# ScalarE makes the copies of the transposed input, and its high and low parts read it in PSUM

## The reference, cut to what matters

```python
h = rmsnorm(x, g_mix_pre)        # x * rsqrt(mean(x*x) + eps) * gain
q_a, k_a, v_a, q_r, k_r, v_r, g_r, gate_a, gate_r = split_in(h @ w_in)
...
x = x + rmsnorm(merged @ w_out, g_mix_post)
```

## Time and profile before

| | |
|---|---|
| median of 3 runs | 982.86 us |
| lowest, highest | 982.62, 986.0 us |
| the profiled execution | 982.29 us |
| its span | 980.6 us |
| its mean granted clock of TensorE | 0.999 |

### The profile page before, as it was taken

How to read it: one execution, slowest core, us unless ns; L and a number is a source line. 1 busy time by engine, 2 the same in 40 slices (tenths; PEclk the granted TensorE clock), 3 DMA queues, 4 the chain that set the end, 5 groups by cost and what they waited for, 6 DMA issues and landing times.

```text
span 980.6 us, 18692 instructions
## 1 busy us (share of the span) xinstructions
PE 973.6 (99%) x7286; PEld 954.4 (97%) x7286; DVE 632.6 (65%) x1246; ACT 396.9 (40%) x695; POOL 85.7 (9%) x140
## 2 busy tenths in 40 slices
PE   9999999999999999999999999999999999999998
PEld 7999999999999999999999999999999999999997
DVE  6554676757665633435458899535996469976772
ACT  4334533434343522223455555424453234544352
POOL 2123212112100000010003000000000000030000
PEclk9999999999999999999999999999999999999999
DMA  8434221222222232246603533521334213366221
GB/s 215 135 114 130 81 68 55 66 76 68 59 68 66 76 92 81 76 127 186 182 3 118 204 86 87 151 66 47 109 99 128 72 48 109 98 202 192 87 55 44
DMA packets 166213, 98.68 MB, mean 101 GB/s; under 512 B 14656, under 2 KB 162528, under 8 KB 165872
## 3 DMA queue, kind: packets, MB, share of 16 engines
q1 hardware_dynamic: 159904, 79.19, 28.6%
q0 software_dynamic: 4336, 16.67, 4.8%
q10 hardware_dynamic: 1888, 1.64, 0.6%
HBM read 86.79 MB, written 10.75 MB: 99 GB/s over the span
## 4 chain that ended last, share of the span: by engine, by line
PE 97%; DVE 1%; DMA 1%; SPq 0%; issue 0%; ACT 0%; DVEq 0%
PE acc L683 37%; PE acc L960 11%; PE acc L961 11%; PE acc L962 11%; PE small L960 6%; PE small L961 6%; PE small L962 6%; PE small L829 1%; PE small L875 1%; PE small L846 1%; PE small L879 1%; PE small L838 1%; PE small L877 1%; PE acc L791 1%; DMA x_row<-in_x_sample 1%; PE small L1117 1%
## 5 line engine op out<-in xcount | busy, mean ns | idle before, releaser
L683 PE MATMUL acc<-xh,whi 128*128 128x288 f32 x720 | 158.9, 302 | 0.1
L683 PE MATMUL acc<-xh,wlo 128*128 128x288 f32 x720 | 153.4, 294 | 0.0
L683 PE MATMUL acc<-xl,whi 128*128 128x288 f32 x720 | 153.4, 294 | 0.0
L1143 ACT ACTIVATE whi<-raw 128x1024 fp32r<-128x1024 f32 (+1 forms) x61 | 61.1, 1002 | 197.7 <-PE acc L683 196.4
L683 PEld LDWEIGHTS acc<-xh,whi 128*128 128x128 f32 x720 | 113.9, 188 | 5.9 <-issue 4.7
L683 PEld LDWEIGHTS acc<-xh,wlo 128*128 128x128 f32 x720 | 115.0, 188 | 0.0
L683 PEld LDWEIGHTS acc<-xl,whi 128*128 128x128 f32 x720 | 115.0, 188 | 0.0
L1965 DVE TENSOR_TENSOR wlo<-raw,whi 128x512 fp32r<-128x512 f32 (+2 forms) x93 | 80.9, 871 | 50.0 <-ACT whi L1359 34.3
L960 PE MATMUL acc<-yh,whi 128*128 128x288 f32 x360 | 107.0, 297 | 0.0
L962 PE MATMUL acc<-yh,wlo 128*128 128x288 f32 x360 | 106.1, 295 | 0.0
L1636 DVE TENSOR_TENSOR wlo<-raw,whi 128x1024 fp32r<-128x1024 f32 (+1 forms) x63 | 73.0, 1158 | 44.4 <-ACT whi L1143 43.4
(11 more groups left out here) (326 smaller groups left out, 2396.1 us busy)
## 6 DMA issues: line engine op xcount, KB each, us to landing
raw<-in_w_in SPq DMA_DIRECT2D x92, 256.0 KB, 3.2
raw<-in_w_ffn_gate SPq DMA_DIRECT2D x44, 256.0 KB, 3.4
raw<-in_w_ffn_up SPq DMA_DIRECT2D x44, 256.0 KB, 4.2
raw<-in_w_ffn_down SPq DMA_DIRECT2D x32, 256.0 KB, 3.7
res<-x_scratch POOLq DMA_DIRECT2D x16, 288.0 KB, 4.2
raw<-in_w_branch_ret SPq DMA_DIRECT2D x16, 256.0 KB, 3.0
raw<-in_w_out SPq DMA_DIRECT2D x16, 256.0 KB, 4.4
raw<-in_w_ffn_down SPq DMA_DIRECT2D x16, 192.0 KB, 3.8
```

What stands on the lines that cost most here:

```text
L683: ins = nc.tensor.matmul(acc[:, a, hf, 0:HALF], w[:, s, at:at + P], x(k)[:, hf * HALF:(hf + 1) * HALF], start=first and n == 0 and m == 0, ...
L1143: nc.scalar.activation(whi[:, s, 0:n], raw[:, s, 0:n], ACT.Copy).then_inc(hi_ready, 1)
```

## The change

PSUM halves get a name, `xt_of(k)`. ScalarE's xh reads the block there instead of in `x_t`, and VectorE's xl too. The copy to `x_t` moves from VectorE to ScalarE: that of block k - 1 stands behind xh of block k and waits until xl of block k - 1 has been made. VectorE copies the gains first. TensorE's hook runs behind the matmuls of unit 0 in a step, not ahead of them.

```diff
+        def xt_of(k):
+            return small[:, 1024 * (k % 2):1024 * (k % 2) + ROWS]
...
                 for step in range(KD + lag):
-                    if before is not None:
-                        before(step)
...
                         if k == KD - 1:
                             ins.then_inc(unit_done, 1)
+                        if n == 0 and before is not None:
+                            before(k)
...
             for k in range(KD):
-                act.wait_ge(xt_copied, k + 1)
-                nc.scalar.activation(xh[:, k, :], x_t[:, k, :], ACT.Copy,
-                                     scale=gains[:, k:k + 1]).then_inc(xh_ready, 1)
+                act.wait_ge(xt_psum, k + 1)
+                nc.scalar.activation(xh[:, k, :], xt_of(k), ACT.Copy, scale=gains[:, k:k + 1]).then_inc(xh_ready, 1)
+                if k > 0:
+                    act.wait_ge(xl_ready, k)
+                    nc.scalar.activation(x_t[:, k - 1, :], xt_of(k - 1), ACT.Copy).then_inc(xt_copied, 1)
                 if k == 0:
                     split_hi(unit(U_KV))
                 elif k == 3:
                     split_hi(unit(U_KV + 1))
                 elif k == KD - 2:
                     row_squares(0)
+            act.wait_ge(xl_ready, KD)
+            nc.scalar.activation(x_t[:, KD - 1, :], xt_of(KD - 1), ACT.Copy).then_inc(xt_copied, 1)
...
-            for k in range(KD + 1):
-                if k < KD:
-                    dve.wait_ge(xt_psum, k + 1)
-                    nc.vector.tensor_copy(x_t[:, k, :], small[:, 1024 * (k % 2):1024 * (k % 2) + ROWS]).then_inc(xt_copied, 1)
+            dve.wait_ge(gain_t, 1)
+            nc.vector.tensor_copy(gains[:, 0:KD], acc[:, 0, 0, 0:KD]).then_inc(gain_ready, 1)
+            dve.wait_ge(gain_ready, 1)
+            for k in range(KD):
+                dve.wait_ge(xh_ready, k + 1)
+                nc.vector.scalar_tensor_tensor(xl[:, k, :], xt_of(k), gains[:, k:k + 1], xh[:, k, :].bitcast(F32),
+                                               ALU.mult, ALU.subtract).then_inc(xl_ready, 1)
                 if k == 0:
-                    dve.wait_ge(gain_t, 1)
-                    nc.vector.tensor_copy(gains[:, 0:KD], acc[:, 0, 0, 0:KD]).then_inc(gain_ready, 1)
-                    dve.wait_ge(gain_ready, 1)
-                if k > 0:
-                    dve.wait_ge(xt_copied, k)
-                    dve.wait_ge(xh_ready, k)
-                    nc.vector.scalar_tensor_tensor(xl[:, k - 1, :], x_t[:, k - 1, :], gains[:, k - 1:k],
-                                                   xh[:, k - 1, :].bitcast(F32), ALU.mult, ALU.subtract).then_inc(xl_ready, 1)
-                if k == 1:
                     split_lo(unit(U_KV))
-                elif k == 4:
+                elif k == 3:
                     split_lo(unit(U_KV + 1))
```

## The result

The changed kernel took 984.07 us in the median of 22 executions (983.35 to 986.56), beside 982.73 us for the kernel before; the ratio is 1.0016, 95% interval 1.001 to 1.0023. So it is slower by 1.3 us, about a fourth of the 0.5% that the prediction called telling. The forecast was 984.1 us. It is closer than its reasons are: the 22 executions are not spread around 984. In 12 of them the granted clock of TensorE was 0.999 or 1.00 and the time 983.35 to 984.2 us (median 983.5); in 10 it was 0.998 or less and the time 985.2 to 986.56 us (median 985.9). The median lies at the upper edge of the first group, because nearly half of the executions fell into the second. That it meets the forecast to 0.03 us is in part luck, and both groups have to be explained. The profiled execution, 985.44 us with a span of 983.8, is one of the second group.

The account below looks back on a forecast made before the run. The prediction took TensorE to bound the kernel. Waits of 0.16, 0.67 and 0.67 us less an old wait of 0.30 made +1.2 us, on the median of 982.86 a forecast of 984.1 us, range 982.0 to 986.5.

Parts of the forecast that it names:

- The bound, and a plain shift behind 32 us: Whole kernel: TensorE bounds, busy 973.6 of 980.6 us; early delay of 1.2 us then carries through as a plain shift.
- The power that I had watched near 36 us: GpSimd's power, ending some 0.4 us ahead of the matmuls reading it; a new wait there would show the forecast wrong.
- Prices of the instructions: Split of x: xh from PSUM 0.74 us, the copy on ScalarE 0.65 us, xl 811 ns.
- The ring: Transposes to the next transposes through ScalarE's xh and the earlier block's copy: 2.31 us a turn.
- T(4) and T(5): TensorE's five transposes each of blocks 4 and 5: forecast to wait 0.67 us each for ScalarE's copy.
- T(6) and T(7): TensorE's transposes of blocks 6 and 7, both units running: forecast no wait, 0.11 us to spare.
- T(2), forecast +0.16: TensorE's transposes of block 2: forecast to start at 10.31 instead of 10.15 us, waiting for block 0's copy.
- The step that the first weights land by 7.92 us: Ahead of the weights' high part on ScalarE: transfers there at 7.92 us at the latest, the high part following at 8.02.
- c(0): The copy of block 0 on ScalarE, behind xh of block 1: forecast to start at 9.62 and end at 10.27 us.
- The clock: Rival: waits around blocks 2 to 7 drop TensorE to 1.2 GHz, about 5 blocks for +4.9 us, 988 or more; chance 0.05.
- The first rival: ScalarE quicker than taken, transposes of blocks 4 and 5 hardly waiting: -0.3 to +0.5 us; chance 0.13.
- the second: ScalarE slower, its PSUM reads taking 1.0 us beside VectorE and TensorE: +3.9 to +4.6 us; chance 0.19.

Follow-up runs that it names:

- e2: The changed kernel with 11 in place of 5 filling products on TensorE ahead of block 2's transposes: 983.76 us.
- e1: The changed kernel with each copy on ScalarE ahead of xh of its own block, and xl reading the copy: 982.93 us.
- e6: The changed kernel with the copies left with VectorE, each right behind xl of its block: 982.54 us.
- e8: The changed kernel with 11 filling products and each of the first seven copies on ScalarE made twice: 987.19 us.
- e4: The kernel before with only TensorE's hook moved behind the first unit's matmuls, copies left with VectorE: 990.84 us.
- e3: The kernel before without the 5 filling products behind block 1's transposes: 985.0 us.
- e5: The changed kernel with TensorE's hook put back ahead of the first unit's matmuls: 984.89 us.
- e10: The same kernel as e7, run again beside e9: 982.24 us.
- e7: The changed kernel with each ScalarE copy ahead of its own block's xh, xl reading the copy, TensorE's old order and 9 filling products: 982.05 us.
- e9: The kernel before with 9 in place of 5 filling products ahead of block 2's transposes, nothing else: 982.69 us.

## Why the prediction was right, and where it was not

*The bound, and a plain shift behind 32 us.* Right: the difference is whole before 32 us. The power that I had watched near 36 us caused no wait.

*Prices of the instructions.* Right. From the groups of 0 to 30 us, after:

```profile
L1172 ACT ACTIVATE xh<-small,gains 128x576 fp32r<-128x576 f32 x8 | 5.9, 739 | 9.8 <-PE small L767 5.8 <-DVE gains L1656 3.8
L1175 ACT ACTIVATE x_t<-small 128x576 f32<-128x576 f32 x7 | 4.5, 642 | 0.0
...
L1660 DVE SCALAR_TENSOR_TENSOR xl<-small,gains,xh 128x576 fp32r<-128x576 f32 x8 | 6.5, 816 | 9.3 <-ACT xh L1172 9.3
```

xh 739 ns where 740 was taken, the copy 642 where 650, xl 816 where 811. The rule of the Trainium skill's "ScalarE: Activation LUTs" (Rules for kernel authors), VectorE for simple arithmetic, names bf16 as its ground. For this fp32 copy out of PSUM it does not hold by price: 642 ns on ScalarE against 757 on VectorE. The change lost on the place of the copy, not on its length.

*The ring.* Right, in place and size, and this is the term that the forecast rested on: waits at T(4) and T(5), none at T(6) and T(7), 2.30 to 2.36 us a turn against 2.31, and 0.66 to 0.72 us a wait against 0.67. Two of its terms were off and cancel: the wake from ScalarE to TensorE took 0.11 us (copy done at 14.49 + 0.64 = 15.13 in e2, weight load at 15.24) and not 0.04, while xh followed T's first weight load by 0.90 (15.24 to 16.14) and not 0.97. e1 and e6 remove the ring and the cost goes; e8 lengthens it and TensorE follows.

*T(2), forecast +0.16.* Mis-sized, and in two terms. The step that the first weights land by 7.92 us was taken from the one execution of before, in which nothing waited for them, and so was the landing of x near 10.1. After, the weights landed at 8.59 in the profiled execution and x near 10.6, and T(2) started 0.81 us late; in e2's the weights landed near 8.2, `whi` began at 8.19 in place of 8.02, c(0) was done at 10.41, and T(2) started at 10.53, 0.39 us late, with x there at 10.2. Against the landing of its own x, T(2) thus waited about 0.3 us for the copy in the profiled execution and some 0.2 in e2's, where the filling products ended near 10.3. The old order had this slack and I gave it away without seeing it.

*The clock.* The rival came in, at another size, and with it one of the signs that I had named for being wrong, a clock under 1.00 before 30 us. I wrote that it needs about five blocks at the low level, made it a case only beyond +4.9 us, and gave it 0.05. In fact the clock fell in 10 of 22 executions, for two blocks and one set of transposes in the profiled one, and the two groups lie 2.4 us apart; in the profiled execution the halved clock is 1.52 us of that. What makes up the rest is not shown; a later T(2) is the nearest candidate. The chance should have gone to a fall at any price, and its price to be added inside "no change". The sign and the class come out the same; the median of 984.07 is made of +1.0 us in 12 executions and +3.4 in 10, against the 982.5 us of the kernel before at full clock, and not of the +1.2 in all that I forecast. Held like against like, the upper group against the 984.6 us of before, it is +1.0 and +1.3; the rest is that the upper group has 10 of 22 executions here and 16 of 75 before.
The Trainium skill's "TensorE: Matmul & The Clock Gate" (HAM oscillation) has repeated waits of TensorE bring the clock down. The trace agrees in direction: here a clock of 0.50 followed the wait of 1.89 us. I had held the 1.00 in the earlier trace rows against it; that row was one execution of before, 16 of 75 others had a clock of 0.998 or less, and a single profile could not have spoken against it.

*The first rival*, ScalarE quicker, and *the second*, slower by contention in PSUM, did not come: the prices above and e6 exclude them.

## What to carry to other kernels

A copy that frees a buffer belongs where its engine reaches it without passing a wait for the next buffer. Put behind the next block's work it closes a ring, and the turn of that ring, worked out from rows, is the time of each step in which the bound engine has less work than that. Before moving a wait, list what stands ahead of it and behind it in its queue on each engine (the weights' transfer ahead of c(0), the copy ahead of xl in e4), and look at more than one execution's clock before calling a gap harmless.

## What the runs showed that I had not expected

A TensorE that stands still early in the program can cost 2 us and more by the low clock, and does not always. The wait ahead of T(2) in each kernel's profiled execution, and how many of its executions had a clock of 0.998 or less:

| kernel | wait ahead of T(2), us | executions with a clock of 0.998 or less |
|---|---|---|
| e3 | 2.39 | 9 of 9 |
| changed | 1.89 | 10 of 22 |
| e5 | 1.52 | 7 of 11 |
| e4 | 0.93 | 4 of 6, with further waits of up to 1.57 us behind it |
| before, beside the experiments | 0.91 | 16 of 75 |
| e6 | 0.62 | 2 of 11 |
| e1 | 0.57 | 1 of 11 |
| e10 | 0.46 | 0 of 11 |
| e8 | 0.39 | 1 of 5, at 987.59 us |
| e7 | 0.38 | 0 of 11 |
| e9 | 0.28 | 1 of 11, at 983.03 us |
| e2 | 0 | 0 of 11 |

On the whole, the longer it stands, the more often the clock falls, though e5 and the changed kernel stand the other way round, and each wait is that of one execution. What decides in one execution stays open, and a profile of one execution, with a clock of 1.00 or 0.50 in it, is one draw of that.
